# Heads seven and eight of the input projection as a fifth pair of seven half-size products

## The reference: what is computed

```python
h = rmsnorm(x, g_norm)
z = einsum('bsd,dn->bsn', h, w_in)      # q, k, v, gate of 16 heads; forget logits; merge gates ma, mb (2048 columns each)
ya = (diff_attention(qa, ka, va) * silu(ga)) @ w_proj_a     # 8 heads with rotary and two maps
yb = (forgetting_attention(qb, kb, vb) * silu(gb)) @ w_proj_b   # 8 heads with a forget bias
m = sigmoid(ma) * ya + sigmoid(mb) * yb
out = rmsnorm(x + m @ w_out, g_final)
```

## Time and profile before

| | |
|---|---|
| Median of three runs | 736.4 us |
| The profiled execution: its time | 736.15 us |
| its span, first to last instruction | 734.0 us |
| Share of the span: PE, DVE, ACT, POOL | 99%, 80%, 61%, 12% |
| Granted TensorE clock, mean | 0.998 |
| Read from HBM | 169.37 MB, 234 GB/s with what is written |

### The profile page before, as it was taken

The page is one execution under the profiler, slowest core; times in us unless marked ns, Lnnn a source line. Parts: engine busy times, 40 slices in busy tenths (PEclk is TensorE's granted clock), DMA queues, the critical chain, the costliest instruction groups (busy, mean ns, idle before and its releaser), DMA issues.

```text
span 734.0 us, 9419 instructions
## 1 busy us (share of the span) xinstructions
PE 724.2 (99%) x3478; PEld 604.3 (82%) x3478; DVE 588.9 (80%) x753; ACT 450.0 (61%) x668; POOL 88.3 (12%) x105
## 2 busy tenths in 40 slices
PE   8999999999999999999999999999999999999995
PEld 6998888888888888888888888888888888888884
DVE  6775798788669788877988886988998667799884
ACT  7963767466656565666656666667666544555562
POOL 0000223103010201010302030202020000001030
PEclk9999999999999999999999999999999999999999
DMA  9778365776956686785576777475777655666853
GB/s 337 209 233 312 144 229 207 247 226 243 331 182 232 214 265 210 269 302 185 215 261 200 251 258 292 173 285 198 231 248 241 211 190 201 279 230 236 288 199 115
DMA packets 48093, 172.10 MB, mean 234 GB/s; under 512 B 5352, under 2 KB 5360, under 8 KB 47536
## 3 DMA queue, kind: packets, MB, share of 16 engines
q1 hardware_dynamic: 46928, 168.12, 66.2%
q10 hardware_dynamic: 864, 1.84, 0.7%
q0 software_dynamic: 256, 1.54, 0.6%
HBM read 169.37 MB, written 2.11 MB: 234 GB/s over the span
## 4 chain that ended last, share of the span: by engine, by line
PE 97%; DMA 1%; issue 1%; ACT 0%; DVE 0%; SPq 0%; DVEq 0%; POOLq 0%; POOL 0%
PE Z L401 28%; PE Z L402 28%; PE Z L416 21%; PE Z L469 7%; PE Z L576 3%; PE A L517 1%; PE A L483 1%; DMA w_raw<-in_w_main 1%; PE B L499 1%; PE Dk L508 1%; PE B L496 1%; PE A L680 0%; PE A L402 0%; PE A L401 0%; PE C L526 0%
## 5 line engine op out<-in xcount | busy, mean ns | idle before, releaser
L935 DVE TENSOR_TENSOR w_lo<-w_raw,w_hi 128x1024 fp32r<-128x1024 f32 (+1 forms) x242 | 296.4, 1231 | 87.0 <-ACT w_hi L702 85.9
L702 ACT ACTIVATE w_hi<-w_raw 128x1024 fp32r<-128x1024 f32 (+1 forms) x241 | 250.0, 1044 | 176.4 <-PE Z L416 132.7
L401 PE MATMUL Z<-w_hi,hT_hi 128*128 128x512 f32 (+2 forms) x680 | 257.5, 382 | 0.0
L402 PE MATMUL Z<-w_hi,hT_lo 128*128 128x512 f32 (+2 forms) x680 | 255.8, 379 | 0.0
L401 PEld LDWEIGHTS Z<-w_hi,hT_hi 128*128 128x128 f32 x680 | 127.8, 188 | 24.6
L402 PEld LDWEIGHTS Z<-w_hi,hT_lo 128*128 128x128 f32 x680 | 127.8, 188 | 23.4
L416 PE MATMUL Z<-w_lo,hT_hi 128*128 128x512 f32 (+2 forms) x576 | 146.5, 377 | 0.0
L416 PEld LDWEIGHTS Z<-w_lo,hT_hi 128*128 128x128 f32 x576 | 104.6, 188 | 19.9
L702 ACT ACTIVATE w_hi<-x_and_g 128x1024 fp32r<-128x1024 f32 x72 | 76.3, 1059 | 58.9 <-DVE x_and_g L950 33.9
L935 DVE TENSOR_TENSOR w_lo<-x_and_g,w_hi 128x1024 fp32r<-128x1024 f32 x72 | 90.0, 1252 | 26.9 <-ACT w_hi L702 25.7
L401 PE MATMUL Z<-w_hi,sum_hi 128*128 128x512 f32 x260 | 102.8, 396 | 0.0
(11 more groups left out here) (212 smaller groups left out, 695.0 us busy)
## 6 DMA issues: line engine op xcount, KB each, us to landing
w_raw<-in_w_main SPq DMA_DIRECT2D x287, 512.0 KB, 4.2
x_and_g<-in_w_main SPq DMA_DIRECT2D x18, 512.0 KB, 6.5
w_raw<-in_w_fl SPq DMA_DIRECT2D x8, 264.0 KB, 2.9
o_T<-in_x SPq DMA_DIRECT2D x1, 2048.0 KB, 8.0
x_and_g<-in_xT SPq DMA_DIRECT2D x4, 256.0 KB, 5.6
gates<-c_rows_dram POOLq DMA_DIRECT2D x1, 1024.0 KB, 7.0
z_sb<-in_g_final SPq DMA_DIRECT2D x1, 1024.0 KB, 10.0
x_and_g<-in_xT ACTq DMA_DIRECT2D x3, 256.0 KB, 7.2
```

The source lines that it names most:

```text
L401: pe.matmul(acc, a_hi, b_hi, start=first, stop=False)
L402: pe.matmul(acc, a_lo, b_hi, start=False, stop=False)
L702: act.activation(w_hi[:, t % RING, 0:cols_of(t)], weights(t), ACT.Copy).then_inc(hi_ready, 1)
L935: dve.tensor_tensor(w_lo[:, t % RING, 0:n], weights(t), w_hi[:, t % RING, 0:n].bitcast(fp32), ALU.subtract).then_inc(lo_ready, 1)
```

## The change

Heads 6 and 7 (the seventh and eighth) no longer have long jobs. Their 2 x 512 columns, the two token halves and the two halves of the input rows are now a first group of seven half-size products, ahead of the four groups of merge gates: 16 long jobs go, 28 short ones come. Its four result blocks land in `gates[:, 2]`, where ACT scales them by `rstd` in place (`gate_in_place` for `g == 0`), and where the attention of heads 6 and 7 reads them (`z_of`, `wait_z`). The merge gates' groups are now 1 to 4. There are 11 head chunks in place of 13, with more short jobs in each: 13 in six of them, 11 in four, 10 in the last. 326 jobs in all, for 314. Heads 3, 4 and 5 go through their attention in the chunk after their own; from head 6 on the attention of a head starts every 15.7 jobs.

```diff
-GROUPS, FORMS, QUARTERS = 4, 7, 4
+GATE_GROUPS, GROUPS, FORMS, QUARTERS = 4, 5, 7, 4
+PAIR_HEADS, PAIR_GROUP = (6, 7), 2
...
-FOX_JOB = MIXED_JOB + 16 * (N_HEADS - 3)
+ALONE = [h for h in range(N_HEADS) if h not in PAIR_HEADS]
+SUMS_IN = [13] * 6 + [11] * 4 + [10]
+STEPS = {13: "hsshshsshshsshshsshss", 11: "hshsshshshsshshshss", 10: "hshshshsshshshshss"}
...
-HEAD_STEPS, SUM_STEPS = (0, 2, 4, 6, 8, 10, 12, 13), (1, 3, 5, 7, 9, 11, 14, 15)
...
+X_ALONE = {**{3 + c: CHUNK_JOB[c + 1] + 4 for c in range(3)}, **{b: CHUNK_JOB[3] + 4 + 157 * (b - 5) // 10 for b in range(6, N_HEADS)}}
...
-O_SPLIT_AT = {FOX_JOB - 20: 0, FOX_JOB - 14: 1, FOX2_JOB + 3: 2, FOX2_JOB + 4: 3}
+O_SPLIT_AT = {FOX_JOB - 18: 0, FOX_JOB - 8: 1, FOX2_JOB + 3: 2, FOX2_JOB + 4: 3}
...
+        def z_of(h):
+            if h in PAIR_HEADS:
+                return gates[:, PAIR_GROUP, :, PAIR_HEADS.index(h), :]
+            return z_sb[:, ALONE.index(h) % Z_SLOTS]
...
+                    n, half = {P1: (0, 0), P5: (1, 0), P6: (1, 1), P3: (1, 1), P7: (0, 0), P4: (0, 1), P2: (0, 1)}[f]
+                    c = PAIR_HEADS[n] if g == 0 else MERGE + 4 * n + g - 1
+                    return w_main[8 * c + 4 * half + q - 4]
...
+                if g == 0:
+                    z_block = z_of(PAIR_HEADS[branch])[:, m]
+                    act.activation(z_block, z_block, ACT.Copy, scale=rstd[:, m:m + 1]).then_inc(pair_ready, 1)
```

More of the change, by code:

```diff
@@ L38 @@
 FL_JOB, VG_JOB, PLAIN_JOB, MIXED_JOB = 8, 16, 20, 28
-FOX_JOB = MIXED_JOB + 16 * (N_HEADS - 3)
+ALONE = [h for h in range(N_HEADS) if h not in PAIR_HEADS]
+SUMS_IN = [13] * 6 + [11] * 4 + [10]
+STEPS = {13: "hsshshsshshsshshsshss", 11: "hshsshshshsshshshss", 10: "hshshshsshshshshss"}
+CHUNK_JOB = [MIXED_JOB]
+for n_sums in SUMS_IN:
+    CHUNK_JOB.append(CHUNK_JOB[-1] + TILES + n_sums)
+FOX_JOB = CHUNK_JOB[-1]
 FOX2_JOB = FOX_JOB + 16
@@ L53 @@
 OUT_DONE = {2: 0, 1: 1, 0: 2}
[L54 removed]
+SUM_JOB = ([CHUNK_JOB[c] + u for c, n_sums in enumerate(SUMS_IN) for u, kind in enumerate(STEPS[n_sums]) if kind == "s"] + [FOX_JOB + u for u in FOX_SUM_STEPS]
            + [OUT_JOB + u for u, kind in enumerate(OUT_ORDER) if kind == "s"])
 SUM_OF = {job: s for s, job in enumerate(SUM_JOB)}
[L57 to L59 removed]
+X_ALONE = {**{3 + c: CHUNK_JOB[c + 1] + 4 for c in range(3)}, **{b: CHUNK_JOB[3] + 4 + 157 * (b - 5) // 10 for b in range(6, N_HEADS)}}
+X_AT = {21: 0, 28: 1, 38: 2, **{job: b for b, job in X_ALONE.items()}, FOX2_JOB + 1: N_HEADS, DIFF_JOB + 1: N_HEADS + 1}
+Y_AT = {25: 0, 33: 1, 43: 2, **{job + 5: b for b, job in X_ALONE.items()}, FOX2_JOB + 5: N_HEADS}
 C_ZERO, C_MASK, C_TRI, C_IDENT, C_ONE = 0, P, 2 * P, 3 * P, 4 * P
@@ L63, with fill_of, head_job @@
 C_ALL = C_LAM + 4 * QK
-def fill_of(c):
+def fill_of(h):
+    c = ALONE.index(h)
     return c if c < 2 else c + 1
-def head_job(c, j):
+def head_job(h, j):
+    c = ALONE.index(h)
     if c == 0:
         return j
-    return PLAIN_JOB + j if c == 2 else MIXED_JOB + 16 * (c - 3) + HEAD_STEPS[j]
+    return PLAIN_JOB + j if c == 2 else CHUNK_JOB[c - 3] + [u for u, kind in enumerate(STEPS[SUMS_IN[c - 3]]) if kind == "h"][j]
 def max_count(heads):
@@ L88 @@
 PARTS_AT = {PLAIN_JOB + 7: 0, MIXED_JOB + 2: 1, MIXED_JOB + 11: 2, MIXED_JOB + 18: 3}
-O_SPLIT_AT = {FOX_JOB - 20: 0, FOX_JOB - 14: 1, FOX2_JOB + 3: 2, FOX2_JOB + 4: 3}
-HEAD_OF = {head_job(c, j): (c, j) for c in range(2, N_HEADS) for j in range(TILES)}
+O_SPLIT_AT = {FOX_JOB - 18: 0, FOX_JOB - 8: 1, FOX2_JOB + 3: 2, FOX2_JOB + 4: 3}
+HEAD_OF = {head_job(c, j): (c, j) for c in ALONE[2:] for j in range(TILES)}
 FOX_OF = {fox_job(n, j): (n, j) for n in range(4) for j in range(4)}
@@ L306, in blocks_of, with wait_z @@
             if g < GROUPS:
-                return [gates[:, g, m, branch, :] for m in range(M_TILES) for branch in range(2)]
+                return [gates[:, PAIR_GROUP if g == 0 else g - 1, m, branch, :] for m in range(M_TILES) for branch in range(2)]
             return [y_sb[:, m, branch * CHUNK:(branch + 1) * CHUNK] for m in range(M_TILES) for branch in range(2)]
+        def z_of(h):
+            if h in PAIR_HEADS:
+                return gates[:, PAIR_GROUP, :, PAIR_HEADS.index(h), :]
+            return z_sb[:, ALONE.index(h) % Z_SLOTS]
+        def wait_z(engine, h):
+            if h in PAIR_HEADS:
+                engine.wait_ge(pair_ready, 4)
+            else:
+                engine.wait_ge(evac[0], fill_of(h) + 1)
+                engine.wait_ge(evac[1], fill_of(h) + 1)
         def form_bank(g, f):
@@ L908, in _ @@
             for part, (m, cols, _) in enumerate(LAST):
-                square(m, 3, cols if part == 0 else LAST_HALVES[0], 29)
+                square(m, 3, cols if part == 0 else LAST_HALVES[0], 27)
                 act.wait_ge(yg_ready, 6)
```

57 lines of the change are left out of this document (26 added, 31 removed).

## The result

| | before | after |
|---|---|---|
| Median of four runs each, same chip | 736.88 us | 742.51 us (739.97 to 743.04) |
| Ratio, with its 95% interval | | 1.0073 [1.0056, 1.0089] |
| The profiled execution: time, span | 736.15, 734.0 us | 739.97, 738.2 us |

The prediction was 733.0 us with a range of 731.0 to 735.8. The measured time lies outside it, on the other side of no change. The profiled execution of after is the fastest of its four; so the trace shows less than the median has lost.

A forecast was written before the change was run, and what follows sets the result against it. The prediction took PE, at 99% of the span, as the bound: 736.15 - 5.4 (fewer matmuls) + 2.0 (PE waiting on DVE) = 732.7 us, or 733.0 as median, 0.25 us above the profiled execution; range 731.0 to 735.8 us.

The forecast's parts named there:

- The saving on PE, 5.4 us: Head projections on PE: 24 matmuls fewer at 0.227 us each, all 5.4 us counting if PE still waits for nobody.
- DVE's work and average: Head chunks: DVE keeps up on each chunk's average; its share rises to 85 or 86%, waits for ACT fall to about 75 us.
- The three places, 2.0 us: Bursts around jobs 154, 202 and 251: PE stands 1.2 + 0.6 + 0.2 = 2.0 us.
- lag: DVE's work less PE's at its peaks: 4.8 us ahead of job 154, 4.4 at 202, 3.7 at 251.
- cover: Time the four-job ring lets DVE run late before PE waits for `w_lo`: 4.75 us for a long job, 5.2 for a short.
- The step that failed: In the three bursts around jobs 154, 202 and 251: one add's wait for its load each, 1 to 2 us.
- POOL's share: DVE passes beside POOL's rotary steps stretch from 1.22 to 1.40 us: below 0.5 us a head, already inside the other allowances.
- Nothing: Token sums for the new first group: ready by step 46, the last wanted at job 55, so no cost.
- Rival 2: Loads tie all ten `P5, P6` and `P7, P4` bursts, PE standing 0.5 to 1.5 us in each: 736 to 746 us; chance 0.23 with Rival 3.
- running sum: DVE's work less PE's over the job order: 3.1 us or less outside the three places, never above 1.9 before.
- Rival 3: DVE bounds whole chunks if a pass costs 1.23 us, not 1.14: 737 us; chance 0.23 together with Rival 2.
- The loads' waits on DVE: DVE's waits for loads over the whole kernel: forecast to rise from 8 to 15 us or more.

The follow-up runs named there:

- adds_half: The kernel with half adds: changed kernel, each weight-block add in the five input-projection groups covering 512 of 1024 columns (computes something else); 730.88 us, ratio 0.9928 to before.
- repeat: The changed kernel run again with nothing altered, for a second profile; 741.29 us, ratio 1.0065 to the kernel before.
- order4: The changed kernel with four raw slots and another job order, picked by a sum counting slot releases, landings and evacuations; 738.28 us, ratio 1.0041 to before.

## Why the prediction was wrong

- **The saving on PE, 5.4 us**: right. The kernel with half adds measures 5.2 of it: 736.12 to 730.88 us.
- **DVE's work and average**: right within a point (84% for 85 or 86; waits for ACT 78 us for 75). That DVE keeps up on the average of every chunk was true and didn't help.
- **The three places, 2.0 us**: right in place and nearly in size (2.5 us), in part by luck. The prediction's reckoning gives almost nothing there without a wait for a load (a lag of 4.8 against a cover of 4.75 us, and 4.4 against 5.2). But with five slots, where DVE waits for no load, 0.65 us stay at job 154 and 0.6 at 202; and at 202 the changed kernel has no wait for a load either (none on DVE between 326 and 547 us) and stands 0.7 us. So DVE's passes alone exceed the cover there, by 0.6 us at both jobs, for 0.05 and none reckoned; the waits for loads, taken as 1 to 2 us a place, account for the other 0.7 us at job 154.
- **The step that failed** is "per place I expect one such wait, 1 to 2 us", with its confinement to three places. The wait of an add for its load was set against the cover only where the computed lag was at its peak. It came at the first add of `P7` in the first two groups as well, 1.07 us (with 0.48 and 0.30 behind it) and 2.22 us. By the prediction's own numbers that is enough: a lag of up to 3.1 us and a wait of 2.2 come to 5.3, over covers of 4.75 to 5.2, with POOL's share still to come. PE stood 2.75 us at jobs 64, 65, 109 and 110, set at nothing. The fifth slot removes these waits altogether, and also those at 248, 251 and 256 and half of that at 154: together 5.1 us of the 6.2 between the two spans (738.2 and 732.0).
- **What is not shown**: that the lateness feeds itself (a late DVE frees its slot late, the load lands late, DVE falls further back), the theory that the fifth slot was tried for. In the second group one wait of 2.22 us and 0.12 us after it are all that the loads add, and in the kernel with half adds, where no `w_lo` holds PE up in the head chunks, DVE waits for loads more often. What is shown is that waits for loads on top of DVE's work exceed the cover, and that either less work or earlier loads mends it.
- **POOL's share was set too low.** The prediction allowed "below 0.5 us" a head for passes stretched beside POOL. Beside the four steps of a forgetting head's bias they come to 1.06 us in the second group. The trace of before had them already, outside the rows read:

```profile
121.12 1.63 DVE L935 TENSOR_TENSOR w_lo<-x_and_g,w_hi 128x1024 fp32r<-128x1024 f32 x1
```

The prediction also held 0.18 us of stretch against 1.2 us of a rotary step. But the row with 1.16 us is four instructions (x4), 0.32 us each; so it doesn't speak against a pass being held up for a whole instruction of POOL, which for one of these would be at most 0.32 us.

- **Cover was taken as full at the start** of each burst. In the first group it wasn't: the excerpt at 146 us shows DVE without a single wait for ACT.
- **Three waits outside the bursts** were set at nothing: the token sums' last splitting pass (job 51, 0.9 us; "Nothing" in the prediction, which asked only whether the sums are ready in time), a bank evacuated late (job 49, 0.9 us), and `fox_gate` (256, 1.2 us). The last two come from a late DVE, by way of ACT's queue and DVE's own. Those at 49 and 51 stay with five slots (0.8 us each), so loads are not their cause.
- **The rivals.** Rival 2 came nearest and was given too little: its 736 to 746 us hold the time, and the loss against the kernel with half adds is 10.4 us (repeat) to 11.6 us (742.5 - 730.9). But it said all ten bursts, and five have stalls; about 3 us of the loss stand in no burst. Of its reasons, landings of 5 us was wrong (they take 4.3), and DVE freeing its slots late once it is late is not shown. The evidence set against it, a running sum of 3.1 us or less outside the three places, left the wait for a load out of the comparison. Rival 3 fell with the distances of starts: 147.99 to 149.13 is 1.14 us again.
- **The loads' waits on DVE** fell short of the forecast: 9.0 us for 15 or more. They are a poor gauge either way, as the 16.4 us of adds_half show.

What stays open: 2.5 us lie between the profiled execution of the change and its median. The size of the waits varies from run to run, in this kernel and in order4 (738.28, 736.72 to 742.06), while adds_half lies within 0.6 us. That without reserve each small variation of a landing reaches PE fits this, but no run varied landings by themselves. Of the 9.6 us in the profile of after, the starts of PE's matmuls set beside those of the kernel with half adds, which has the same order, put 9.1 us at the places of the table: each stall is about 0.1 us longer than in it, since after a wait one more start comes 0.34 us behind the last in place of 0.23. The rest, 0.5 us, is not placed.

## What to carry to other kernels

An engine at 80% that feeds one at 99% has its reserve in the ring between them, and the reserve must be worked out with the loads in the loop: slot freed, landing, pass, slot freed. The longest wait for a load that the trace shows belongs in the comparison with the cover at every burst, not only at the worst ones. Before a change that trades work of the bound for work of its feeder, look whether one more slot can be had: here it took the same change from 0.7% slower to 0.2% faster, while of four other orders and placements with four slots one gained 2 to 3 us and three gained nothing. And a stand of PE can cost more than its length: behind those of 2.2 and 3.2 us there was a stretch at the lower clock.

## What the runs showed that was not expected

- A fifth raw slot of 512 KB is worth 7 us in the changed kernel and nothing (1.0005 [0.9995, 1.0014]) in the one before, though both wait for loads about as long on DVE (9.0 and 8.4 us).
- A pass of DVE, 1.22 us alone, took up to 1.63 us beside POOL's steps (at 238 us); 1.40 was the longest in the rows read before.
- PE stood 3.2 us in one kernel and 2.2 us in another, and its granted clock then was at the lower level for 6.8 and 3.4 us.
- Half the columns per load shortened the landing only from 4.3 to 3.0 us.
